# Decoder trunk of two layers: a head's scores moved beside the preceding head's recurrence, keys first, input gates in two passes

## What is computed

```python
qkv, z, beta_logit, a_logit = jnp.split(x @ w_in, [GDN_CONV, GDN_CONV + GDN_V, GDN_CONV + GDN_V + H], axis=-1)
qkv = _causal_conv_silu(qkv, conv_w)                 # 4 taps along time
q, k, v = ...                                        # l2norm on q and k
beta = sigmoid(beta_logit);  g = -exp(a_log) * softplus(a_logit + dt_bias);  gc = cumsum(g) in a chunk
lmat = strict_lower(kb @ k^T * decay);  uw = solve(I + lmat, [v * beta, kb * exp(gc)])
qk = lower(q @ k^T * decay)
# for every chunk in turn:
v_new = u - w @ state;  o = q_dec @ state + qk @ v_new
state = state * exp(gl) + k_dec^T @ v_new
o = rmsnorm(o) * silu(z);  y = o @ w_out
```

## Time and profile before

| | us |
|---|---|
| median of 3 runs | 1070.25 |
| lowest, highest | 1068.92, 1070.43 |
| the profiled execution | 1068.92 |
| its span, from first to last instruction | 1067.2 |
| PE busy in it | 1032.7 (97%) |
| DVE busy | 702.0 (66%) |
| ACT busy | 498.0 (47%) |
| POOL busy | 213.9 (20%) |

### The profile page before, as it was taken

One profiled execution on the slowest core, in us unless ns is written; L12 is line 12 of the kernel. 1 busy time (PEld: TensorE's weight loads), 2 busy tenths in 40 slices (PEclk: granted clock), 3 DMA queues, 4 the chain that ended last, 5 costly groups with the idle time before them and its releaser, 6 DMA issues. The chain is left out here.

```text
span 1067.2 us, 17846 instructions
## 1 busy us (share of the span) xinstructions
PE 1032.7 (97%) x6325; PEld 841.3 (79%) x6325; DVE 702.0 (66%) x1650; ACT 498.0 (47%) x1388; POOL 213.9 (20%) x569
## 2 busy tenths in 40 slices
PE   7999999999999999999999999999999999999996
PEld 6788777888888778888888888888877777777885
DVE  4476757676767676755456877535367877789765
ACT  4464656575656566644354112202156566567000
POOL 1007380717172726352000000000100000000000
PEclk9999999999999999999999999999999999999998
DMA  6122302222121222213114211202001000012201
GB/s 202 51 61 73 93 23 57 59 49 67 35 81 35 61 54 62 50 46 110 40 41 144 93 60 42 87 1 69 20 1 37 25 21 21 21 60 102 96 40 60
DMA packets 83985, 62.67 MB, mean 59 GB/s; under 512 B 32108, under 2 KB 74156, under 8 KB 83896
## 3 DMA queue, kind: packets, MB, share of 16 engines
q1 hardware_dynamic: 49576, 44.68, 13.8%
q10 hardware_dynamic: 34320, 16.84, 6.2%
HBM read 55.18 MB, written 6.32 MB: 58 GB/s over the span
## 5 line engine op out<-in xcount | busy, mean ns | idle before, releaser
L666 PE MATMUL ps<-act_hi,w_hi 128*128 128x512 f32 x528 | 232.2, 440 | 0.0
L666 PE MATMUL ps<-act_hi,w_lo 128*128 128x512 f32 x528 | 207.6, 393 | 0.0
L666 PE MATMUL ps<-act_lo,w_hi 128*128 128x512 f32 x528 | 206.5, 391 | 0.0
L617 POOL TENSOR_TENSOR rank<-inverse,tok 128x60 f32<-128x60 f32 (+24 forms) x248 | 93.6, 377 | 190.4 <-DMA tok<-blocks_in 171.6
L1453 DVE SCALAR_TENSOR_TENSOR tok<-xs,convw,tok 128x512 f32<-128x512 f32 x144 | 110.9, 770 | 13.9 <-ACT xs L1143 12.5
L666 PEld LDWEIGHTS ps<-act_hi,w_lo 128*128 128x128 f32 x528 | 99.1, 188 | 22.0
L666 PEld LDWEIGHTS ps<-act_hi,w_hi 128*128 128x128 f32 x528 | 100.1, 190 | 11.1
L666 PEld LDWEIGHTS ps<-act_lo,w_hi 128*128 128x128 f32 x528 | 100.3, 190 | 9.7
L851 PE MATMUL ps<-wo_hi,act_hi 128*128 128x512 f32 x256 | 101.0, 395 | 1.0 <-DVE wo_lo L1511 1.0
L620 POOL TENSOR_TENSOR inverse<-inverse,rank 128x60 f32<-128x60 f32 (+24 forms) x248 | 96.3, 388 | 19.4
L851 PE MATMUL ps<-wo_lo,act_hi 128*128 128x512 f32 x256 | 100.1, 391 | 0.0
(11 more groups left out here) (258 smaller groups left out, 2172.8 us busy)
## 6 DMA issues: line engine op xcount, KB each, us to landing
w_raw<-in_a_w_in ACTq DMA_DIRECT2D x32, 512.0 KB, 4.2
tok<-in_x SPq DMA_DIRECT2D x8, 512.0 KB, 7.1
decay<-gc_rows SPq DMA_DIRECT2D x8, 512.0 KB, 5.1
tok<-blocks_in SPq DMA_DIRECT2D x32, 128.0 KB, 2.7
xres<-in_x SPq DMA_DIRECT2D x8, 512.0 KB, 3.4
ws_raw<-in_b_w_in SPq DMA_DIRECT2D x16, 256.0 KB, 2.6
z_raw<-in_b_w_in SPq DMA_DIRECT2D x8, 512.0 KB, 3.8
out<-yr SPq DMA_DIRECT2D x8, 512.0 KB, 2.6
```

The costliest lines, as they stand in the source:

```text
L617: inner.next(pool.tensor_tensor(part, inverse[:, 0:rows, m:m + 1].broadcast_to([P, rows, w]), blocks[:, m:m + 1, m + 1:32].broadcast_to([P ...
L666: mm = pe.matmul(ps[:, g % 2, :], lhs[:, k, :], rhs[:, k, HALF * b:HALF * (b + 1)], start=(i == 0), stop=(i == GROUP - 1))
```

## The change

- **Keys first.** `channel_tile` exchanges q and k: each head projects k, then q, then v. TK (transposed keys) moves to place 0.54 of a head, TQ behind the scores (1.12).
- **Scores and recurrence.** In the three tables everything from the levels to the output comes earlier: the first level from place 2.32 to 1.882, the first step of the recurrence from 2.415 to 1.984. The scores move from 0.9953 to 1.139 (plus up to 0.19 of `LATE_TURN`) to 0.9505 to 1.038, so that the scores of head h+1 stand directly behind the last level of head h, among the first steps of its recurrence. The shifts by head are nearly all zero.
- **The mask** of the next head stands in the middle of the inverse, behind its 13th step (`MASK_AT`), and the next step waits for it.
- **Waits.** The semaphores on which transpositions, scores and levels wait follow the new order of the PSUM banks.
- **The input gates.** The low part of the gate weights stands in 16 more columns of the high tile; two passes (activation high, activation low) give all products, and the four parts are added on VectorE. 32 matmuls (L664 of the changed kernel) take the place of 48. The first 16 stand between the transpositions of the last tiles of x. The convolution rows are loaded behind the fourth tile of x.

In the changed kernel the lines are: projection L684, scores L782 and L783, levels L810, L815 with L817, L820 and L823, recurrence L833 and L834, L846, L854 and L856, output transposition L874, GpSimd's steps L623 and L626, mask L604.

```diff
+AT_PE = {"TK": [0.5401],
+          "M": [0.9505, 0.9629, 0.9753, 0.9879, 1, 1.013, 1.025, 1.038],
+          "TQ": [1.12],
...
+          "L": [1.882, 1.903, 1.919, 1.939],
...
+AT_DVE = {"TK": [0.5382],
...
+          "X": [1.831],
...
-            return (w % 3) * GH + w // 3 if w < QKV_TILES else w
+            return (1, 0, 2)[w % 3] * GH + w // 3 if w < QKV_TILES else w
...
+                pool.wait_ge(s_mask, h + 1)
...
-                if h + 1 < GH:
-                    mask_decay(h + 1)
+                    if m == MASK_AT and h + 1 < GH:
+                        mask_decay(h + 1)
...
+            def project_input_gates(b, k0):
+                for k in range(k0, k0 + NK // 2):
+                    for j in range(2):
+                        mm = pe.matmul(ps[:, INPUT_GATE_BANKS[b], :], w_hi[1][:, k, :],
+                                       (act_hi, act_lo)[j][:, k, HALF * b:HALF * (b + 1)],
+                                       start=(k == 0 and j == 0), stop=(k == NK - 1 and j == 1))
+                if k0:
+                    mm.then_inc(s_gates, 1)
...
                 if i == 0:
                     pe.wait_ge(s_xr, h + 1)
-                    pe.wait_ge(s_m, NT * min(h + 2, GH))
+                    pe.wait_ge(s_sq, NT * (h + 1))
```

More of the change, by code:

```diff
@@ L152, in plan @@
                     continue
-                late = 0.0 if kind == "TQ" else LATE_TURN[h] if kind in TURN_KINDS else LATE_SCAN[max(h, 0)]
+                late = LATE_TURN[h] if kind in TURN_KINDS else LATE_SCAN[max(h, 0)]
                 name, c = STEPS[i] if kind == "S" else (kind, i)
@@ L682, in turn_input @@
                     mm.then_inc(s_xtr, 1)
[L684 removed]
+            for t in range(NT // 2 + 1):
                 turn_input(t)
+            pe.wait_ge(s_whi, 1)
+            pe.wait_ge(s_wlo, 1)
             pe.wait_ge(s_xlo, NT)
[L687 to L689 removed]
+            project_input_gates(0, 0)
+            turn_input(NT // 2 + 1)
+            project_input_gates(0, NK // 2)
+            turn_input(NT // 2 + 2)
+            turn_input(NT // 2 + 3)
+            pe.wait_ge(s_crow, 48)
             for w in range(QKV_TILES):
@@ L702, in _ @@
             mm.then_inc(s_gtr, 1)
-            for q in range(0, GROUP, STEP):
+            for q in range(2 * STEP, GROUP, STEP):
                 project(0, q)
+            for q in range(0, 3 * STEP, STEP):
+                project(1, q)
             pe.wait_ge(s_gd, 3)
             g_all = sc["g"][:, :, :].rearrange("p h c -> p (h c)")
-            pe.matmul(ps[:, 3, 128:192], tri, g_all, start=True, stop=True)
-            pe.matmul(ps[:, 3, 192:256], tri[:, P - 1:P].broadcast_to([P, P]), g_all,
+            pe.matmul(ps[:, 3, 256:320], tri, g_all, start=True, stop=True)
@@ L709, in _, with turn_k @@
+            pe.matmul(ps[:, 3, 320:384], tri[:, P - 1:P].broadcast_to([P, P]), g_all,
                       start=True, stop=True).then_inc(s_gc, 1)
+            for q in range(3 * STEP, FIRST - GROUP, STEP):
+                project(1, q)
             pe.wait_ge(s_gd, 5)
-            pe.transpose(ps[0:64, 3, 256:384], sc["gc"][:, :, :].rearrange("p h c -> p (h c)"), ident[:, :])\
+            pe.transpose(ps[0:64, 3, 384:512], sc["gc"][:, :, :].rearrange("p h c -> p (h c)"), ident[:, :])\
               .then_inc(s_gct, 1)
-            def turn_q(h):
+            def turn_k(h):
@@ L774, in level @@
                     if h + 1 < GH:
-                        pe.wait_ge(s_tev, 2 * h + 3)
+                        pe.wait_ge(s_kd, 2 * h + 3)
+                        pe.wait_ge(s_sk, NT * (h + 1) + 4)
+                    else:
+                        pe.wait_ge(s_tev, 2 * GH)
                 elif i == 2:
@@ L834, in transpose_out @@
                 pe.wait_ge(s_oscaled, h + 1)
-                pe.wait_ge(s_m, NT * min(h + 3, GH))
-                if h + 3 > GH:
+                if h + 2 < GH:
+                    pe.wait_ge(s_kd, 2 * h + 6)
+                    pe.wait_ge(s_sk, NT * (h + 3))
+                    pe.wait_ge(s_sq, NT * (h + 2))
+                else:
                     pe.wait_ge(s_tev, 2 * GH)
+                    pe.wait_ge(s_sq, NT * GH)
+                    if h + 1 == GH:
+                        pe.wait_ge(s_ut, 2 * GH)
                 if h:
@@ L870, in _ @@
             for kind, a, b in PE_PLAN:
-                if kind == "mm" and a > 0:
+                if kind == "mm" and GROUP * a + b >= FIRST:
                     project(a, b)
```

135 lines of the change are left out of this document (77 added, 58 removed), and 39 rows, old and new, of tables (AT_ACT, AT_DVE).

## The result

The changed kernel took 1200.87 us (median of 4 runs, 1199.59 to 1205.51), the kernel before 1069.95; the ratio is 1.123 (95% interval 1.120 to 1.126). The forecast was 1145 us, with a range up to 1180. The direction and the place were right, the size was not: 131 us were lost instead of 75.

The account below looks back on a forecast made before the run. TensorE, now busy 97%, was to wait for the inverse's round trip: 47.5 us trip, 14.9 back and 2 for the clock made 64.4 a head, the stage ending 74.7 us later: 1145 us, range 1100 to 1180.

Parts of the forecast that it names:

- The bound now, and the loop: TensorE's longest wait moves to the first level, for the inverse: about 20 us in head 0, 7 to 11 in heads 1 to 6.
- part 4: Behind the wait at the first level, TensorE works at 1.2 GHz: 2 us a head taken, bounds nothing and 4 us.
- part 2: Inverse's round trip, from a head's last score product done (T0) to its first level: 47.5 us, 50 in head 0.
- Part 1: Start: 32 gate matmuls instead of 48; first projection group at 23.5 instead of 31.74, 8.2 us won, uncertain by 1.5.
- 35.5 us until GpSimd is done: First leg of the inverse's round trip, from the last score product to GpSimd's end, read from head 3 of the kernel before.
- term (c): VectorE's VS and OS now fall beside GpSimd's inverse: 0.8 us taken, bounds nothing and 2.4; 1.7 by the skill's rule.
- Head 0's 50 us: Head 0's round trip from last score product to first level, with its slower transfers: 50 us against 47.5 in other heads.
- Part 3: From a head's first level through the next head's scores to their last product (T0): 14.9 us, 13.5 to 16.
- The sum: Whole kernel: 64.4 us for each further head (47.5 + 14.9 + 2), stage end 74.7 us later, 1145 us in all.
- (D): Rival for the loop: trip 50 us, clock 4 us a head, head 0 in 53: 1180 us; chance 0.11 for above 1170.
- (B): Rival for the loop: trip 45.2 us, head 0 in 47, no clock loss: 1110 us; chance 0.17 for 1090 to 1122.
- (A): Rival for the loop: the inverse's trip fits, TensorE never waits long, not slower: about 1058 us; chance 0.05.

Follow-up runs that it names:

- e3: Changed kernel with 15 of GpSimd's 31 inverse steps left out in every head, so part of the inverse is not computed: 1067.65 us.
- e2: Changed kernel with ScalarE's fetches of the next weight tile 14 projection matmuls later, away from the reads of the blocks: 1187.39 us.
- e6: Changed kernel with VectorE's instruction VS (L1598) moved from place 1.647 to 1.84, behind X, where GpSimd is idle: 1199.15 us.
- e1: Changed kernel with 42 to 78 idle matmuls, results unread, ahead of each head's first level, before TensorE's wait there: 1182.96 us.
- e7: Changed kernel with both idle matmuls (32 to 82 a head) ahead of the first levels and the weight tile's fetch 14 matmuls later: 1149.42 us.
- e8: Changed kernel with 15 of GpSimd's 31 inverse steps left out in heads 1 to 7 and 26 in head 0, its mask moved up: 1054.91 us.
- e5: Kernel before with the new start alone (input gates in two passes, convolution rows earlier); tables, key order, waits and mask as before: 1063.93 us.

## Why the prediction was right or wrong

**The bound now, and the loop: right.** The wait at L810 behind VectorE's transposition, about 20 us in head 0 (18.6) and 7 to 11 in the others (11 to 13.7), the vanished waits for the scores' products, the longer inverse (31 to 33 us; 32.3) came as said. e3 shows that 38 us is the point from which the trip decides. Of the 58 us missing in the span, some 31 lie in the way back and the last stretch (part 4), some 25 in the trips (part 2) and 2 at the start.

**Part 1, the start: right, 1.4 us off.** The first group of projection stood at 24.94, not 23.5, inside the 1.5 us given.

**Part 2, the trip: 3.8 us short.** The step that failed here is the sentence "35.5 us until GpSimd is done", taken over from head 3 of before. It holds the reads of the blocks at that kernel's distance from the fetch of the weight tile: there the fetch was issued 1.8 us behind the reads (239.50 against 237.72, the two rows below), in the changed order 0.5 us. I had walked past ScalarE's fetches when I moved T0, and they are issued by place in the projection too. It costs 2.8 us at GpSimd's start in head 3, and e2 wins 2.5 us a head back. The inverse itself was 0.6 us longer than forecast (32.3 against 28.3 + 1.1 + 1.5 + 0.8 = 31.7), and the legs behind it 0.3 us. Within the inverse term (c), VS and OS at 0.8 us, was mis-sized: they hold GpSimd for 0.9 and 1.0 us, 1.9 in all, so the other terms were 0.5 too high together. Only VS was tried by a run (e6); the price of OS is read from the trace alone. Head 0's 50 us has no sum behind it: its legs of before, 46.5 + 3.2 + 1.5, are 51.2 without the mask. It came at 47.9, nearer to the forecast than to these legs, which is luck.

The reads in SyncE's queue and the fetch in ScalarE's, kernel before:

```profile
237.72 1.71 SPq L505 DMA_DIRECT2D tok<-blocks_in  x4
...
239.50 0.37 ACTq L1084 DMA_DIRECT2D w_raw<-in_a_w_in  x1
```

By the rule of the Trainium skill (SBUF — State Buffer, section Who interferes with whom) that stood beside term (c), a GpSimd instruction that reads SBUF contends with a VectorE instruction that has two inputs in SBUF, and the one issued later is blocked until the other ends. This case's trace agrees where VS and OS began first: 1.20 and 1.30 us beside them against 0.26 without. The 1.7 us that I had worked out by it was the better price.

**Part 3, from the level to T0: right.** 14.9 us was forecast, 15.0 to 16.0 measured wherever the clock stayed at 1.00 (e1, e3, e7, e8).

**Part 4, the clock: wrong, and the largest miss.** This term of the sum is the step that failed most. I saw that the clock would fall, but took 2 us a head with 4 as the upper bound, "half of the 8 us that PE's own work takes behind the wait". It costs 20.8 - 15.3 = 5.5 us (the means of the changed kernel and of e1's four heads at 1.00). The bound was wrong in itself: PE ran at 1.2 GHz for 13.5 us behind the level, and the half-speed stretch lies on the levels and scores on which all of the way back hangs. The projection matmuls stand 336.06 - 335.63 = 0.43 us apart there, against 0.227:

```profile
335.63 0.63 PE L684 MATMUL ps<-act_lo,w_hi 128*128 128x512 f32 x1
336.06 0.63 PE L684 MATMUL ps<-act_hi,w_lo 128*128 128x512 f32 x1
```

Since the way back is part of the loop, each of these 5.5 us is paid in full. A safe upper bound, as an estimate without a row for the length of the low clock, would have been the whole way back at half speed, 14.9 us more; a range up to 1145 + 8 x (14.9 - 2) = 1248 would have held the time.

**The sum.** With the measured trip, 51.3, and 14.9 + 5.5 for the way back, the same sum gives 71.7 us a head; first levels were 71.3 to 73.1 us apart up to head 6. The form of the sum was right, two of its terms were not.

**The rivals.** (D) had the right direction (trip 50, clock 4 us) and still ended 21 us short; it had 0.11. (B), in which GpSimd is left alone and the clock costs nothing, failed on both counts. (A) was the estimate of the order without the trip, 1058 us; e8, with most of head 0's inverse and half of the others' left out, gives 1054.9.

## What to carry to other kernels

When work is reordered so that a round trip closes a loop (the request stands behind the answer to the one before), its whole length is paid in every turn. Here each wait of TensorE within it was paid a second time, with 5.5 us at 1.2 GHz behind it. Take each leg of the trip from a row together with what else was on the transfer queues at that moment, since the new order moves the neighbours too. And split a change before judging it: here the start was worth 5 us to keep, and the order cost 137.

## What the runs showed of the hardware that I had not expected

- Behind head 3's wait the granted clock stayed at 0.50 through 13.5 us of full work (331.46 to some 345). The loss did not go with the length of the wait: after waits of 8 to 18.6 us the way back was always 20 to 22 us.
- Short waits can do it as well, and their length alone doesn't tell which: in e1 the clock fell behind waits of 1.6, 2.8 and 2.9 us and held behind others of 0.7 to 1.9. In e6, and in e1 too, it also fell for some 3 us at the gate projection (between 21 and 26 us), where PE had just run small transpositions of 4x4 and waited 0.3 us; in the changed kernel's execution the same place kept 1.00. What decides between them stays open.
- Matmuls whose result nobody reads keep the clock up in TensorE's waits, and GpSimd's inverse doesn't notice them: it took 32.3 to 33.4 us in heads 1 to 6 of e7 and 32.6 to 33.1 in e2.
- A fetch of 512 KB issued half a microsecond behind four reads of 128 KB made the last of these land 5.7 us after its issue instead of 2.9. The same shows inside e5: in head 2, with the fetch 0.6 us behind the reads, it landed after 5.4 us, in head 1, with 1.4 us between, after 3.1. It is not the only thing that delays them: in head 6 of the kernel before no fetch was issued within 8 us, and the landing took 4.0 us.
